# Four landing buffers for the last gate's half pieces, and down's last inner tiles finished by token tile

## What is computed

```python
mod = silu(c) @ w_mod[l] + b_mod[l]
sh1, sc1, g1, sh2, sc2, g2 = jnp.split(mod[:, None, :], N_MOD, axis=-1)
...
x = x + g1 * rms_norm(merged @ w_out[l], post_mix_norm[l])
h = rms_norm(x, pre_ffn_norm[l]) * (1.0 + sc2) + sh2
y = conv_ffn(h, w_ffn_up[l], ffn_conv_w[l], ffn_conv_b[l], w_ffn_down[l])
x = x + g2 * rms_norm(y, post_ffn_norm[l])
```

## Time and profile before

| | |
|---|---|
| median of 3 runs | 2833.53 us (2830.37 to 2833.89) |
| the profiled execution | 2836.03 us, its span 2834.4 us |
| mean granted TensorE clock | 0.989 |
| busy: PE, DVE, ACT, POOL | 2752.1, 1882.8, 1063.8, 102.0 us |
| moved by DMA | 400.79 MB |

### The profile page before, as it was taken

How to read it: one execution, slowest core, us unless ns; L and a number is a source line. 1 busy time by engine, 2 the same in 40 slices (tenths; PEclk the granted TensorE clock), 3 DMA queues, 4 the chain that set the end, 5 groups by cost and what they waited for, 6 DMA issues and landing times.

```text
span 2834.4 us, 43664 instructions
## 1 busy us (share of the span) xinstructions
PE 2752.1 (97%) x15886; PEld 2426.2 (86%) x15886; DVE 1882.8 (66%) x2523; ACT 1063.8 (38%) x1428; POOL 102.0 (4%) x189
## 2 busy tenths in 40 slices
PE   5999999999999999999989999999999999999997
PEld 4788888888788888878768999999999998888886
DVE  7857777777756666535567788888888884334334
ACT  4344444444522222232243344444444443223223
POOL 0030000000000000002210000000000000000000
PEclk8999999999999999999989999999999999999999
DMA  9842222222277777646643443434343436522222
GB/s 362 309 119 74 79 75 81 72 80 82 67 216 208 216 218 217 200 149 201 200 149 100 134 128 106 129 104 129 104 129 104 129 89 209 205 96 97 96 96 96
DMA packets 454080, 400.79 MB, mean 141 GB/s; under 512 B 21579, under 2 KB 378210, under 8 KB 451184
## 3 DMA queue, kind: packets, MB, share of 16 engines
q1 hardware_dynamic: 429920, 340.83, 40.4%
q0 software_dynamic: 14176, 54.69, 5.6%
q10 hardware_dynamic: 9904, 4.26, 0.6%
HBM read 378.73 MB, written 20.99 MB: 141 GB/s over the span
## 4 chain that ended last, share of the span: by engine, by line
PE 92%; DVE 3%; DMA 2%; issue 1%; ACT 1%; SPq 0%; POOL 0%; ACTq 0%; DVEq 0%; POOLq 0%
PE acc_bank L613 19%; PE acc_bank L615 19%; PE acc_bank L614 19%; PE two_banks L613 3%; PE two_banks L614 3%; PE two_banks L615 3%; PE bank_pb L613 2%; PE bank_pb L614 2%; PE bank_pb L615 2%; PE bank_tb L613 2%; PE bank_ta L613 2%; PE bank_tb L615 2%; PE bank_tb L614 2%; PE bank_ta L614 2%; PE bank_ta L615 2%
## 5 line engine op out<-in xcount | busy, mean ns | idle before, releaser
L589 DVE TENSOR_TENSOR w_lo<-raw,w_hi 128x1024 fp32r<-128x1024 f32 x309 | 377.7, 1223 | 686.6 <-ACT w_hi L583 686.5
L583 ACT CAST w_hi<-raw 128x1024 fp32r<-128x1024 f32 x309 | 324.3, 1050 | 917.4 <-PE acc_bank L615 427.8
L613 PE MATMUL acc_bank<-h_hi,w_hi 128*128 128x512 f32 x1268 | 503.4, 397 | 6.4 <-DVE h_lo L1604 6.4
L615 PE MATMUL acc_bank<-h_hi,w_lo 128*128 128x512 f32 x1268 | 495.0, 390 | 0.0
L614 PE MATMUL acc_bank<-h_lo,w_hi 128*128 128x512 f32 x1268 | 494.5, 390 | 0.0
L613 PEld LDWEIGHTS acc_bank<-h_hi,w_hi 128*128 128x128 f32 x1268 | 238.8, 188 | 53.3 <-issue 6.5
L615 PEld LDWEIGHTS acc_bank<-h_hi,w_lo 128*128 128x128 f32 x1268 | 238.4, 188 | 50.5
L614 PEld LDWEIGHTS acc_bank<-h_lo,w_hi 128*128 128x128 f32 x1268 | 238.9, 188 | 47.2
L613 PE MATMUL acc_bank<-h_hi,s_hi 128*128 128x256 f32 x608 | 172.1, 283 | 0.0
L614 PE MATMUL acc_bank<-h_lo,s_hi 128*128 128x256 f32 x608 | 172.1, 283 | 0.0
L615 PE MATMUL acc_bank<-h_hi,s_lo 128*128 128x256 f32 x608 | 172.1, 283 | 0.0
(11 more groups left out here) (493 smaller groups left out, 6641.7 us busy)
## 6 DMA issues: line engine op xcount, KB each, us to landing
raw<-in_w_in_dram SPq DMA_DIRECT2D x148, 512.0 KB, 4.1
raw<-in_w_mod_dram SPq DMA_DIRECT2D x96, 512.0 KB, 4.5
raw<-in_w_ffn_up_dram SPq DMA_DIRECT2D x96, 512.0 KB, 4.5
raw<-in_w_ffn_down_dram SPq DMA_DIRECT2D x86, 512.0 KB, 3.6
raw_odd<-in_w_ffn_up_dram SPq DMA_DIRECT2D x76, 512.0 KB, 4.5
mods_low<-in_w_mod_dram SPq DMA_DIRECT2D x32, 512.0 KB, 9.5
raw<-in_w_out_dram SPq DMA_DIRECT2D x32, 512.0 KB, 4.1
small<-in_w_mod_dram POOLq DMA_DIRECT2D x64, 256.0 KB, 4.0
```

Source lines behind the costliest of these rows:

```text
L583: act.copy(w_pair(g, gp)[0][:], raw[n % RAW][:]).then_inc(hi_ready, 1)
L589: dve.tensor_tensor(w_l[:], raw[n % RAW][:], w_h[:].bitcast(F32), ALU.subtract).then_inc(lo_ready, 1)
L613: pe.matmul(o, stat[0], mov[0], start=start, stop=False)
L615: return pe.matmul(o, stat[1], mov[0], start=False, stop=stop)
```

## The change

It has two parts. The first lets the half pieces of the last gate land in four buffers rather than two: the last 512 columns of the four tiles of `y1`. POOL no longer waits for the merge ahead of them, and the three loads of x's token tiles are moved from the start of the product to behind half pieces 20, 36 and 52. The second part handles the last four inner tiles of the second sweep of the down product. Their split weights and activations are written to places of their own (`end_hi`, `end_lo`, `end_ah`, `end_al`, over activation tiles that have been read by then), without waiting for PE. PE goes over the four once for each bank, so that a token tile is complete after 24 matmuls. The multiply-add of the last token tile and its store are done in two halves of 1024 columns.

```diff
--- before.py
+++ after.py
@@ -169,7 +169,9 @@
             + [(f"y{n}", [P, 8, H], F32) for n in (21, 11, 12, 22)],
             [("t_home", [P, 6, 8, H], F32R), ("raw_odd", [P, 4, PIECE], F32), ("sums", [P, 2, PIECE], F32),
              ("s_hi2", [P, PIECE], F32R), ("s_lo2", [P, PIECE], F32R), ("act_ring", [P, 3, T], F32),
-             ("s_hi3", [P, PIECE], F32R), ("s_lo3", [P, PIECE], F32R), ("gelu_out", [P, T], F32)])
+             ("s_hi3", [P, PIECE], F32R), ("s_lo3", [P, PIECE], F32R), ("gelu_out", [P, T], F32)],
+            [("end_hi", [P, 4, PIECE], F32R), ("end_lo", [P, 4, PIECE], F32R),
+             ("end_ah", [P, 4, T], F32R), ("end_al", [P, 4, T], F32R)])
         x_in, xT, square_junk, vec_rows = (RO[0][n] for n in ("x_in", "xT", "square_junk", "vec_rows"))
         partial = RO[0]["partial"]
         MODS_SLOTS = ([RH[3]["mods_hi"][:, i] for i in range(2)] + [RH[3]["mods_lo"][:, i] for i in range(2)]
@@ -186,9 +188,11 @@
         y1, m_hi, m_lo = RO[4]["y1"], RO[4]["m_hi"], RO[4]["m_lo"]
         x2_last = RO[5]["x2_last"]
         act_t, gain2 = RO[6]["act"], RO[6]["gain2"]
+        end_hi, end_lo, end_ah, end_al = (RO[10][n] for n in ("end_hi", "end_lo", "end_ah", "end_al"))
         y_raw = {n: RO[8][f"y{n}"] for n in (11, 12, 21, 22)}
         raw_odd, w_sums, gelu_out = RO[9]["raw_odd"], RO[9]["sums"], RO[9]["gelu_out"]
         g2_sums = x_again[:, TT - 1, :]
+        g2_in = [y1[:, t, 3 * 512:] for t in range(TT)]
         raw = [sb(f"raw{i}", [P, PIECE]) for i in range(RAW)]
         w_hi = [sb(f"w_hi{i}", [P, PIECE], F32R) for i in range(SPL)]
         w_lo = [sb(f"w_lo{i}", [P, PIECE], F32R) for i in range(SPL)]
@@ -205,6 +209,8 @@
                 return RH[1]["out_hi"][:, g - OUT_KEPT - 1], RH[1]["out_lo"][:, g - OUT_KEPT - 1]
             if g == P4 - 1:
                 return w_hi[OUT_KEPT % SPL - 1], w_lo[OUT_KEPT % SPL - 1]
+            if g >= END - 4:
+                return end_hi[:, g - END + 4], end_lo[:, g - END + 4]
             if P4 <= g < P4 + 2:
                 return RO[5]["up_hi"][:, g - P4], RO[5]["up_lo"][:, g - P4]
             return w_hi[g % SPL], w_lo[g % SPL]
@@ -213,6 +219,8 @@
 
             if P5 <= g < P5 + 2:
                 return g - 3
+            if g >= END - 4 and not looped:
+                return 0
             if not looped:
                 if OUT_KEPT < g < P4 - 1:
                     return P3
@@ -274,7 +282,7 @@
         DOWN_BANKS = [A[0][:], A[1][:], A[2][:], PB[:], SC0, SC1, TA[:], TB[:]]
 
 
-        g2_landed = [sem(f"g2_landed{i}") for i in range(2)]
+        g2_landed = [sem(f"g2_landed{i}") for i in range(4)]
         t_step = sem("t_step")
         sums_ready, mid_out, halves = sem("sums_ready"), sem("mid_out"), sem("halves")
         act_stored = [sem(f"act_stored{i}") for i in range(2)]
@@ -569,10 +577,11 @@
                     load(N5 + base + i, 0, "w", P5 + base + i, 0, w_down_t[:, k0:k0 + 1, s * 1024:s * 1024 + 1024])
                 run(N5 + base + 3, (FB - 3) // 4, [("w", P5 + base + 3 + i, 4) for i in range(4)],
                     lambda it, i, s=s: (lambda r: w_down_t[:, ds(r, 1), s * 1024:s * 1024 + 1024], it * 4 + i))
-            for i in range(TT):
+            for i in range(TT + 1):
                 sp.wait_ge(out_ready, i + 1)
-                sp.dma_start(out_rows[i], y2[:, i, :]).then_inc(out_stored, 16)
-            sp.wait_ge(out_stored, 16 * TT)
+                r, cols = (i, slice(0, D)) if i < TT - 1 else (TT - 1, slice((i - TT + 1) * D // 2, (i - TT + 2) * D // 2))
+                sp.dma_start(out_rows[r][:, cols], y2[:, r, cols]).then_inc(out_stored, 16)
+            sp.wait_ge(out_stored, 16 * (TT + 1))
 
 
         def split_hi(act, g, n, it=0, gp=0, np_=0):
@@ -1078,7 +1087,23 @@
                     for i in range(4):
                         down(base + 3 + i, it, sweep, False, False)
                 for u in range(39, 43):
-                    down(base + u, 0, sweep, False, u == 42)
+                    if sweep == 0:
+                        down(base + u, 0, sweep, False, u == 42)
+
+            for t4 in range(TT):
+                for ch in range(2):
+                    for j in range(4):
+                        g = END - 4 + j
+                        if t4 == 0 and ch == 0:
+                            pe.wait_ge(lo_ready, g + 1)
+                            pe.wait_ge(al_ready, 2 * FB - 3 + j)
+                        wh, wl = weights(g, 1)
+                        mm = three(DOWN_BANKS[2 * t4 + ch], (end_ah[:, j, t4 * P:(t4 + 1) * P], end_al[:, j, t4 * P:(t4 + 1) * P]),
+                                   (wh[:, 0, ch * 512:(ch + 1) * 512], wl[:, 0, ch * 512:(ch + 1) * 512]), False, j == 3)
+                        if t4 == TT - 1 and ch == 1:
+                            mm.then_inc(multiplied, 1)
+                    if t4 < TT - 1 or ch == 0:
+                        mm.then_inc(y_done, 1)
 
 
         @block.scalar
@@ -1517,11 +1542,16 @@
                     down(base + u)
                     if u == 0 and s == 1:
                         sweep_out_act(act, 0)
-                with act.Fori(0, 10) as it:
+                with act.Fori(0, 10 - s) as it:
                     if s == 0:
                         act.wait_ge(back_landed, it * 16 + 16)
                     for i in range(4):
                         down(base + 3 + i, it)
+            act.wait_ge(al_ready, FB + 27)
+            for j in range(4):
+                g, u = END - 4 + j, FB + 39 + j
+                split_hi(act, g, N5 + u)
+                act.copy(end_ah[:, j, :], act_t[:, u - FB - 3, :]).then_inc(ah_ready, 1)
 
             for i in range(TT):
                 sweep_out_act(act, 1, (2 * i, 2 * i + 1))
@@ -1953,11 +1983,11 @@
 
                 q, kt = divmod(j, KT)
                 dst = g2_sums[:, 512 * q:512 * q + 512]
-                dve.wait_ge(g2_landed[j % 2], 16 * (j // 2 + 1))
+                dve.wait_ge(g2_landed[j % 4], 16 * (j // 4 + 1))
                 if kt == 0:
-                    return TS(dst, small[:, 2 + j % 2, :], csil[:, 0:1], None, ALU.mult).then_inc(mod_ops, 1)
+                    return TS(dst, g2_in[j % 4], csil[:, 0:1], None, ALU.mult).then_inc(mod_ops, 1)
                 dve.wait_ge(mod_ops, 2 * MODS_LAST + j)
-                return STT(dst, small[:, 2 + j % 2, :], csil[:, kt:kt + 1], dst, ALU.mult, ALU.add).then_inc(mod_ops, 1)
+                return STT(dst, g2_in[j % 4], csil[:, kt:kt + 1], dst, ALU.mult, ALU.add).then_inc(mod_ops, 1)
 
             for i in range(2, 34):
                 if i < 32:
@@ -2203,9 +2233,14 @@
                     if u == 0 and s == 1:
                         dve.wait_ge(gain_landed, 32)
                         sweep_out(0)
-                with dve.Fori(0, 10) as it:
+                with dve.Fori(0, 10 - s) as it:
                     for i in range(4):
                         down(base + 3 + i, it)
+            for j in range(4):
+                g, u = END - 4 + j, FB + 39 + j
+                split_lo(dve, g, N5 + u)
+                dve.wait_ge(ah_ready, u + 1)
+                TTe(end_al[:, j, :], act_t[:, u - FB - 3, :], end_ah[:, j, :].bitcast(F32), ALU.subtract).then_inc(al_ready, 1)
 
             for i in range(TT + 1):
                 if i < TT:
@@ -2219,7 +2254,10 @@
                     if j == 0:
                         dve.wait_ge(back_landed, 64 + 4 * ACT_HOME)
                     dve.wait_ge(y2_out, 8 + 2 * i)
-                    STT(y2[:, j, :], y2[:, j, :], rms[:, j:j + 1], x2_again[:, j, :], ALU.mult, ALU.add).then_inc(out_ready, 1)
+                    for c in (range(1) if i < TT else range(2)):
+                        w = D if i < TT else D // 2
+                        STT(y2[:, j, c * w:c * w + w], y2[:, j, c * w:c * w + w], rms[:, j:j + 1], x2_again[:, j, c * w:c * w + w],
+                            ALU.mult, ALU.add).then_inc(out_ready, 1)
 
 
         @block.gpsimd
@@ -2283,20 +2321,20 @@
             pool.wait_ge(v_stored, 8 * 16)
 
             pool.wait_ge(multiplied, P3)
-            for i in range(TT - 1):
-                pool.dma_start(x_again[:, i, :], x_rows[i]).then_inc(x3_landed, 16)
             pool.wait_ge(grow_ready, 1)
             pool.dma_start(g_scr[0:KT], small[0:KT, 0, 0:P]).then_inc(grow_stored, 16)
             pool.wait_ge(grow_stored, 16)
             row = lambda a: g_scr[a * KT:(a + 1) * KT, :].rearrange("n p -> (n p)").partition_broadcast(P)
             pool.dma_start(gain1[:], row(0)).then_inc(gain_landed, 16)
-            pool.wait_ge(merged_ready, KT)
             for j in range(4 * KT):
                 q, kt = divmod(j, KT)
-                if j >= 2:
-                    pool.wait_ge(mod_ops, 2 * MODS_LAST + j - 1)
+                if j >= 4:
+                    pool.wait_ge(mod_ops, 2 * MODS_LAST + j - 3)
                 col = (MOD_G2 + 4 * q) * P
-                pool.dma_start(small[:, 2 + j % 2, :], w_mod_t[:, kt, col:col + 512]).then_inc(g2_landed[j % 2], 16)
```

(4 more changed lines are left out.)

## The result

The changed kernel takes 2817.36 us in the median of 6 runs (2814.78 to 2819.27), the one before 2833.71 us in 6 runs beside it (2830.37 to 2841.17). The ratio is 0.9936, with a 95% interval of 0.9925 to 0.9946: 0.64% faster, some 18 us. The forecast was 2814.7 in a range of 2810 to 2823. The profiled execution took 2817.47 us, its span 2816.0 us.

What follows compares the result with a forecast made beforehand. PE, busy 97% of the span, was taken as the bound, so only its waits and the tail count: 5.8 + 4.0 + 9.0 = 18.8 us off the 2833.53 median gives 2814.7, range 2810 to 2822.9.

Steps and rivals of the forecast that it cites:

- The end: After T, the end of PE's last matmul: tail falls from 16.7 to 10.9 us, 5.8 less.
- Place one: 1253 to 1284 us, product's start: without x loads there, PE's stall and slow clock stretch go, 4.0 of 4.24 us.
- Place two: 1407 to 1439 us, PE's last group: four buffers let the gate's sums start earlier, 9.0 us gained.
- rival (a): Last group: transfers bind, landings of 6 us and a slow stretch leave 4.8 of 9.0 us; 2818.9 us, chance 0.13.
- (b): Product's start: the stall stays since DMA is shared with weight loads; gain 14.8, 2818.7 us, chance 0.12.
- (c): Tail: half stores don't overlap, the second starts when the first has landed; 2.2 us more, 2816.9, chance 0.05.
- (d): After the sums: x2 stores and x's last tile don't follow them, only the end gains; 2827.7 and up, chance 0.05.
- (e): Half pieces 21, 37, 53: x loads make them land beyond their 10.9 us lead, PE runs dry; 2844 us, chance 0.03.
- (f): Last 96 matmuls: chains of 12 into one bank run at 0.43 us pitch, costing 19 us; 2834, chance 0.02.

Runs made afterwards that it cites:

- whole_last2: Changed kernel with the last token tile's multiply-add and store whole again, run a second time for its profile: 2818.19 us (one run).
- own_root: Changed kernel with each token tile's root, reciprocal and multiply-add right behind its own two products: 2813.75 us, ratio to before 0.9923.
- x_bunched: Changed kernel with all three x loads behind half piece 52: 2821.18 us, ratio to before 0.9953.
- g2_only: Kernel before with the first part alone (four buffers, moved x loads, no wait for the merge): 2822.88 us, ratio to before 0.9956.
- g2_early: Changed kernel with three half pieces behind most early splits, so only splits stand in the last group: 2812.76 us, ratio to before 0.9922.
- both_moved: Changed kernel with the new orders of own_root and g2_early together: 2809.02 us, ratio to before 0.9901.
- sums_first: both_moved with the last gate's sums ahead of the first kept token tile instead of the third: 2808.31 us, ratio to before 0.9899.
- x_at_start: Changed kernel with the three x loads back at the start of the product, four buffers kept: 2822.48 us, ratio to before 0.9949.
- tail_only: Changed kernel with its first part undone, only the second part left: 2831.31 us, ratio to before 0.9984.
- two_buffers: Changed kernel with two landing buffers instead of four, x loads still behind half pieces 20, 36, 52: 2829.14 us, ratio to before 0.9979.

## Why the prediction was right, point by point

**The end (5.8 forecast, 5.79 measured).** Each step came within 0.05 us: product at T + 0.83 (the same), tile 2's multiply-add at T + 1.69 (1.68), the last operation to T + 6.63 (6.6; the steps as written, 4.14 and twice 1.28, give 6.7), end at T + 10.92 (10.9). Right for the stated reason: the transfers of the last three stores are one stretch, and whole_last2 shows that the halves aren't what shortens the tail. Twelve matmuls in a row into one bank cost nothing: the turned order starts at 2783.16 and its 96 matmuls keep the pitch of 0.23 us without a wait. The Trainium skill ("DMA: Bandwidth & Descriptors", section Bandwidth) has the rule to batch transfers to 1 MiB or more. Breaking it did no harm here: one half store alone landed in 2.7 us and a whole one in 3.9, so by an estimate from these two about 1.5 us of each is fixed, but it passes beside the transfer ahead.

**Place one (4.0 forecast, 2.87 measured).** The mechanism held, all of it: the store landed sooner, the stall is gone, and pieces are 5.44 apart. The term came out too large by what happened at the head of the stretch. PE's first piece with `w_out` runs at half clock in both kernels, 7 matmuls long before, 14 after. The timeline of PE after:

```profile
1255.08 0.63 PE L623 MATMUL acc_bank<-w_lo,m_hi 128*128 128x512 f32 x1
...
1259.77 0.63 PE L622 MATMUL acc_bank<-w_hi,m_hi 128*128 128x512 f32 x1
...
1260.62 0.39 PE L624 MATMUL acc_bank<-w_hi,m_lo 128*128 128x512 f32 x1
```

Seven matmuls at 0.43 instead of 0.23 us are 1.4 us, and 2.87 + 1.4 is 4.3, the full price of the stall. Two other kernels show it without this sum: whole_last2 and own_root have the changed kernel's code there and seven slow matmuls, like the kernel before, and took 143.32 and 143.20, 4.2 and 4.3 less than before. All kernels here without the x loads at the start took between 143.18 and 144.67, with 6 to 14 slow matmuls, so the change is worth 2.9 to 4.4 us there against this one execution of before. That the two profiles give 2.87 is chance. I had counted the slow stretch behind the stall, not that the one at the start can vary.

**Place two (9.0 forecast, 8.09 measured).** The step that was mis-sized is the landing time. I took 4.0 us; with up to four loads in flight and the weight pieces beside them the halves behind the x load took 5.0 to 5.7. The longest of them, and the x load:

```profile
y<-in_w_mod_dram POOLq DMA_DIRECT2D x1, 256.0 KB, 5.7
...
x_again<-in_x_dram POOLq DMA_DIRECT2D x1, 1024.0 KB, 7.3
```

The x load ahead of half 53 landed in 7.3 us (5.0 taken), half 53 in 7.4, and DVE waited 0.38 us for it where I had 1.3 to spare, and 0.43 and 0.59 us for the next two pairs ahead of PE's last wanted split. PE's waits were 1.52 and 1.66 instead of 1.0 and 1.3. No slow stretch came ahead of the sums. So rival (a), the transfers bind, was partly true: it took one of the four microseconds that I gave it. The sums start 12.45 us earlier in the span, where 13.5 was forecast, and 1.62 of it is the spread ahead of the change. The claim that all behind the sums moves with them held, but that it held to 0.03 us is luck: the same stretch took 1378.1 to 1379.6 in the other profiles of the table.

**The rivals.** (b) fell: no stall in place one. (c) fell: the stores overlap. (d) fell: 1378.25 and 1378.22, so what stands behind the sums followed them. (e) did not occur, but x_bunched shows its mechanism; the lead of half 53 was some 7 us, not the 10.9 that I gave all three places, since in the last group DVE no longer waits for PE's pace. At half pieces 21 and 37 no wait shows. (f) fell: it would have cost 19 us in the last 96 matmuls, and they keep their pitch.

**The sum.** 18.8 forecast against 18.4 between the spans, of which 1.6 is the spread ahead of the change: 16.8 belong to it. The median moved by 16.35, and by the ratio by 18.1 us. The changed median lies 2.7 above the 2814.7 forecast; the two terms that came out short, 1.1 and 0.9 us, are 2.0 of it in the profiles, and the rest is within the spread of the runs.

## What to carry to other kernels

Price a stall together with what it does to the clock behind it and with the program order of every engine behind it: three x loads that nobody waited for cost about 4 us, as a small store and a chain of half pieces stood behind them in one queue. When a tail consists of turns of work, see whose turn the program puts first: here the mended order (each tile's finish behind its own products) was worth 3.1 us, and halving the last store, while another store was ahead of it, nothing. And when a stretch is short of an engine and of transfers at once, don't deepen the buffers alone but move work out of it into a stretch with room: that gave another 4 to 6 us.

## What the runs showed of the hardware that I had not expected

The 32 one-column matmuls of the sums took 3.62 to 3.73 us in g2_only, g2_early, both_moved, sums_first, x_bunched, whole_last2 and own_root, 4.65 in the changed kernel, 4.79 before, 5.00 in x_at_start, 5.87 in tail_only and 6.02 in two_buffers. The time goes with the granted clock over the sums: 0.96 to 1.00 in the first seven, then 0.77, 0.75, 0.72, 0.61 and 0.59. Neither the order ahead of them alone nor the wait just ahead sets it: the changed kernel and own_root have the same code and no wait there, and took 4.65 and 3.73. And the same event, a short stop of PE ahead of its first matmul with `w_out` (1.55 us in each profile), was followed by 6 or 7 matmuls at half clock in eight of the twelve profiles and by 12 to 14 in the other four. So single profiles of one place can differ by some 1.5 us from this alone.
